# Rotary turn of retention heads: a permutation product on TensorE or two half-partition instructions on VectorE

## What is computed

```
half = t.shape[-1] // 2
ang = positions.astype(jnp.float32)[..., None] * freq
...
t1 = t[..., :half].astype(jnp.float32)
t2 = t[..., half:].astype(jnp.float32)
return jnp.concatenate([t1 * cos - t2 * sin, t1 * sin + t2 * cos], axis=-1).astype(t.dtype)
...
q = _rotary(q, positions)
k = _rotary(k, positions) * (dh ** -0.5)
...
s = jnp.einsum('bhid,bhjd->bhij', qc, kc) * decay_intra
```

## Time and profile before

| | us |
|---|---|
| median of 3 runs | 3482.7 |
| lowest and highest | 3477.58, 3488.25 |
| the profiled execution: its time | 3476.79 |
| the profiled execution: its span | 3474.8 |
| TensorE busy | 3343.4 |
| VectorE busy | 1779.1 |
| ScalarE busy | 1196.5 |
| GpSimd busy | 411.3 |

### The profile page before, as it was taken

How to read it: one execution, slowest core, us unless ns; L and a number is a source line. 1 busy time by engine, 2 the same in 40 slices (tenths; PEclk the granted TensorE clock), 3 DMA queues, 4 the chain that set the end, 5 groups by cost and what they waited for, 6 DMA issues and landing times.

```text
span 3474.8 us, 44141 instructions
## 1 busy us (share of the span) xinstructions
PE 3343.4 (96%) x18394; PEld 2598.4 (75%) x18394; DVE 1779.1 (51%) x2532; ACT 1196.5 (34%) x1884; POOL 411.3 (12%) x318
## 2 busy tenths in 40 slices
PE   5999999899999899999999999999999999999999
PEld 4776778576677788887777777888777887678887
DVE  6854454744436744336767554333554334563333
ACT  3344432433443422224333342222343223442221
POOL 0000011000000311002322111100101011011110
PEclk8999999999999999999999999999999999999999
DMA  5631122222122333324200013332322323023232
GB/s 208 214 110 61 49 97 91 72 80 61 55 76 71 103 103 91 97 86 124 69 18 3 26 47 118 94 95 85 100 79 91 96 90 94 13 61 97 91 97 85
DMA packets 83909, 295.44 MB, mean 85 GB/s; under 512 B 9472, under 2 KB 12800, under 8 KB 81664
## 3 DMA queue, kind: packets, MB, share of 16 engines
q1 hardware_dynamic: 78384, 270.61, 24.9%
q10 hardware_dynamic: 5328, 22.02, 1.8%
HBM read 283.94 MB, written 8.65 MB: 84 GB/s over the span
## 4 chain that ended last, share of the span: by engine, by line
PE 85%; DVE 9%; ACT 2%; issue 2%; POOL 1%; DMA 0%; ACTq 0%; DVEq 0%; POOLq 0%
PE acc L475 68%; DVE w_lo L386 1%; PE acc L1464 1%; PE acc L3219 1%; PE acc L2445 1%; ACT w_hi L379 1%; DVE square_sums L2904 1%; PE aux L1745 1%; PE aux L3183 1%; PE acc L1778 1%; DVE ssd_ex L1366 1%; PE acc L2449 1%; PE acc L2435 1%; PE aux L1765 1%; PE aux L2402 1%
## 5 line engine op out<-in xcount | busy, mean ns | idle before, releaser
L475 PE MATMUL acc<-op_hi,w_hi 128*128 128x512 f32 x2624 | 1099.2, 419 | 37.9 <-DVE w_lo L386 16.8
L475 PE MATMUL acc<-op_lo,w_hi 128*128 128x512 f32 x2624 | 1040.4, 396 | 0.0
L475 PE MATMUL acc<-op_hi,w_lo 128*128 128x512 f32 x2624 | 1040.0, 396 | 0.0
L379 ACT ACTIVATE w_hi<-raw 128x1024 fp32r<-128x1024 f32 (+2 forms) x476 | 494.8, 1039 | 1582.4 <-PE acc L475 1554.6
L386 DVE TENSOR_TENSOR w_lo<-raw,w_hi 128x1024 fp32r<-128x1024 f32 (+2 forms) x476 | 576.8, 1212 | 289.9 <-ACT w_hi L379 289.5
L475 PEld LDWEIGHTS acc<-op_hi,w_hi 128*128 128x128 f32 x2624 | 495.2, 189 | 219.3 <-issue 82.7
L475 PEld LDWEIGHTS acc<-op_hi,w_lo 128*128 128x128 f32 x2624 | 495.2, 189 | 119.5
L475 PEld LDWEIGHTS acc<-op_lo,w_hi 128*128 128x128 f32 x2624 | 496.3, 189 | 115.0 <-issue 11.5
L475 PE MATMUL acc<-ffn_hi,w_hi 128*128 128x512 f32 x800 | 316.7, 396 | 0.0
L475 PE MATMUL acc<-ffn_lo,w_hi 128*128 128x512 f32 x800 | 316.3, 395 | 0.0
L475 PE MATMUL acc<-ffn_hi,w_lo 128*128 128x512 f32 x800 | 316.3, 395 | 0.0
(11 more groups left out here) (580 smaller groups left out, 3915.6 us busy)
## 6 DMA issues: line engine op xcount, KB each, us to landing
raw<-in_w SPq DMA_DIRECT2D x436, 512.0 KB, 3.5
late_ada<-in_ada ACTq DMA_DIRECT2D x32, 512.0 KB, 3.8
raw<-in_w SPq DMA_DIRECT2D x32, 384.0 KB, 3.1
ada<-in_ada ACTq DMA_DIRECT2D x4, 1024.0 KB, 14.9
ada<-in_ada SPq DMA_DIRECT2D x4, 1024.0 KB, 21.8
x_mid<-x SPq DMA_DIRECT2D x16, 256.0 KB, 3.4
x<-x_mid SPq DMA_DIRECT2D x2, 2048.0 KB, 7.8
skew<-rel_rows SPq DMA_DIRECT2D x12, 192.0 KB, 2.8
```

The lines of the kernel that those rows point to most:

```text
L379: act.activation(self.w_hi[g % 2][:, 0:k, :], self.raw[s][:, 0:k, :], ACT.Copy).then_inc(self.split_hi.handle, 1)
L475: mm = pe.matmul(self.bank(s, g), w[:, k, :], a[:, k, 0:s.n], start=(k == 0 and q == 0), stop=(k == k_tiles - 1 and q == 2))
```

## The change

The product with `rot` goes, and with it the signal `swapped` and the use of the banks `aux[0]` and `aux[1]` by the rotation. VectorE instead reads `qk` itself, in two instructions of 64 partitions each: one reads the second half of the head and the second half of `sin` and writes minus their product to the first 64 partitions of `part2`, and one reads the first halves and writes their product to partitions 64 to 127. The first of them waits for what the product with `rot` waited for (queries and keys there, attention done). The addition and POOL's product stay. VectorE's model times lie 2.3 apart now instead of 1.6, and begin at 0.4. POOL's stay 1.6 apart. The score's stays at `start + 20`.

```diff
@@ class Ret, pe
-        def rotations():
-            for j in range(2 * RET_HEADS):
-                yield self.start + 1.6 * j
-                if j == 0:
-                    pe.wait_ge(*self.qk_ready)
-                    pe.wait_ge(*self.fox.done())
-                if j >= 2:
-                    pe.wait_ge(*self.sined.ge(j - 1))
-                pe.matmul(core.aux[j % 2][:, :], core.c("rot"), qk[:, j, :], start=True,
-                          stop=True).then_inc(*self.swapped.inc())
...
@@ class Ret, dve
         def rotations():
             for j in range(2 * RET_HEADS):
-                yield self.start + 1.6 * j + 1.4
-                dve.wait_ge(*self.swapped.ge(j + 1))
+                yield self.start + 2.3 * j + 0.4
+                if j == 0:
+                    dve.wait_ge(*self.qk_ready)
+                    dve.wait_ge(*self.fox.done())
                 if j >= 2:
                     dve.wait_ge(*self.turned.ge(j - 1))
-                dve.tensor_tensor(self.part2[:, j % 2, :], core.aux[j % 2][:, :], core.sin[:, :],
+                upper, lower = slice(HD, P), slice(0, HD)
+                dve.scalar_tensor_tensor(out=self.part2[lower, j % 2, :], in0=qk[upper, j, :], scalar=-1.0,
+                                         in1=core.sin[upper, :], op0=ALU.mult, op1=ALU.mult)
+                dve.tensor_tensor(self.part2[upper, j % 2, :], qk[lower, j, :], core.sin[lower, :],
                                   ALU.mult).then_inc(*self.sined.inc())
                 dve.wait_ge(*self.sined.ge(j + 1))
                 dve.wait_ge(*self.cosed.ge(j + 1))
```

More of the change, by code:

```diff
@@ L1872, in __init__ @@
         self.loaded = core.share("ret_decay", 16)
-        self.swapped, self.cosed, self.sined, self.turned = (core.share("rot_" + s, n) for s in (
-            "swapped", "cos", "sin", "done"))
+        self.cosed, self.sined, self.turned = (core.share("rot_" + s, n) for s in ("cos", "sin", "done"))
         self.units = [(h, jt) for h in range(RET_HEADS) for jt in range(NT)]
@@ L1972, in spreads @@
                 mm.then_inc(*self.spread.inc())
-        return rotations(), scores(), values(), means(), spreads()
+        return scores(), values(), means(), spreads()
     def norm_time(self, h):
```

## The result

| | before | after |
|---|---|---|
| median of 16 runs each, us | 3482.57 (3477.29 to 3500.5) | 3500.03 (3490.27 to 3508.95) |
| ratio | | 1.0049, interval 1.0038 to 1.0059 |
| span of the profiled execution, us | 3474.8 | 3499.4 |
| mean granted clock of TensorE | 0.983 | 0.977 |
| L379 to L379 around the rotations, layer 1 and layer 2, us | 31.06, 31.04 | 37.90, 37.91 |

What follows compares the result with a forecast made beforehand. It took TensorE as the bound before, and VectorE's eight rotations after: 17.04 us of rotations, 4.12 POOL, 2.40 copies and 2.52 tile work put the score 6.5 us later; +13.2 us for two layers gave 3496, range 3486 to 3504.

Steps and rivals of the forecast that it cites:

- VectorE becomes the bound: In each layer's rotations, the score waits for VectorE's eighth rotation, 26.08 us after VectorE is free at 492.95.
- A rotation at 2.13 us: On VectorE, two half instructions at 0.68 us and an addition at 0.69, without overlapping starts: 2.13 us, before 1.33.
- POOL's turns at 4.12 us: Per layer, VectorE's two-input instructions take turns with POOL's cosine product and lose 4.12 us in all.
- rival of POOL and the half instructions passing each other: Half instructions run beside POOL undelayed: 3.0 us a layer, 3489, or 3485.5 with overlapping starts; chance 0.18.
- TensorE idle in a new place: Before the score, TensorE waits nearly 12 us at the third unit of transposes for the first copy, L1883.
- Nothing for the clock at the score: TensorE at half clock after its wait reaches the score half a microsecond late; nothing was taken for this.
- The rival with more lost: Low clock past the score (3502.5) or POOL costing its whole 1.12 us in all six cases (3501); chance 0.14.
- +6.5 at the score, +6.6 at the first product with the values: In each layer the score moves from 512.66 to 519.2, the first product with the values from 515.56 to 522.2.
- the same distance from the score to the layer's end: Behind the score TensorE has the same work as before, so the distance to the layer's end stays unchanged.
- The relief counts for nothing: TensorE's saved 8 us a layer gain nothing, since the score waits for VectorE; the opposing rival, 3467, had chance 0.02.
- The sum carried over to the median: Two layers' +13.2 us, added to the median of 3482.7, give 3495.9; the difference carries over unchanged.
- VectorE is 2.7 us behind TensorE: In the kernel before, VectorE's eighth rotation ends at 509.93, 2.7 us before the score that waits for it.

Runs made afterwards that it cites:

- pool_no_read: The changed kernel with POOL's cosine product replaced by a memset of the same tile: ratio to before 1.0020, layers 2.80 and 2.83 us longer than before.
- same_half: The changed kernel with both half instructions reading and writing partitions 0 to 63, the turn left out: each layer 5.58 us longer than before; no ratio.
- one_full: The changed kernel with one 128-partition instruction in place of the two half ones, the swap left out: ratio to before 1.0013, layers +1.40 and +1.64 us.
- old_pace: The changed kernel with VectorE's model times as before the change (1.6 apart, from 1.4): ratio to before 1.0059, layers +8.22 and +9.40 us.
- by_head2: The changed kernel, all work kept, rotations ordered by head and spread out, copies given room: ratio to before 0.9967, layers -7.35 and -7.33 us.
- before_idle: The kernel before with two unused reciprocals on VectorE ahead of its fifth rotation, nothing taken off TensorE: ratio to before 1.0044, layers +7.96 and +8.45 us.

## Why the prediction came out as it did

Point by point, by the prediction's steps:

- **VectorE becomes the bound.** Right. It predicted 26.08 us from VectorE's being free to the end of the eighth rotation; in after it is 494.90 (the end of L386) to 520.99, 26.09. That it fits to 0.01 us is luck: POOL's turns were 0.1 us less than summed, and the rest 0.1 us more (22.06 in pool_no_read for 21.96).
- **A rotation at 2.13 us.** Right. From 494.93 to 497.07 it is 2.14. The half instruction has 0.69 us for the 0.68 assumed, and same_half shows that the missing overlap is due to the change of partitions.
- **POOL's turns at 4.12 us.** Right within 0.1 us: 4.03 by after against pool_no_read (26.09 - 22.06). By the rows, L2014 lost 0.99 us (0.98 predicted) in rotation 2, POOL took 1.79 (1.7 to 1.8), and L2012 of rotation 7 lost 1.28 - 0.69 = 0.59 (0.63). One reading was ill chosen: L2021 at 501.86 was not beside POOL, which had ended at 501.39. The L2021 at 504.32, inside POOL's 503.34 to 505.52, shows that it never waited, with 0.68 us. The rival of POOL and the half instructions passing each other falls.
- **TensorE idle in a new place.** Right: nearly 12 us predicted, 11.81 measured, and for the copy that was named.
- **Nothing for the clock at the score.** Right, but by a narrow margin. The prediction's own arithmetic had TensorE half a microsecond too late and let that pass, and TensorE came 0.3 us early for two reasons that it didn't have: the slow matmuls lasted 5.6 us for the 6.65 of the earlier trace rows, and the two units of transposes were 0.43 us each for 0.60. one_full and old_pace show what happens without the margin: the score comes 1.3 and 2.1 us behind VectorE (in old_pace 0.3 of them would be there at full clock too, 515.04 + 5.8 against 520.5).
- **The rival with more lost.** The measured 3500 lies close to its 3501 and 3502.5, but neither of its mechanisms came about. The clock was back at full before the score, and POOL cost 4.0 us and not 6 x 1.12.
- **+6.5 at the score, +6.6 at the first product with the values.** The score stands at 521.05 - 1.95 = 519.10 (519.2 predicted), the product with the values at 524.26 - 1.95 = 522.31 (522.2), 6.75 us later than before; the layer ends 6.85 later. So the sign "the same distance from the score to the layer's end" didn't hold to the tenth: 8.17 us for 7.77, 0.3 of them up to the product with the values. The 0.25 us that are missing a layer make 13.7 instead of 13.2.
- **The relief counts for nothing.** Right in this order of work: one_full has it alone and is not faster. by_head2 shows that this holds for the order and not for the chip. There the relief is worth 7.3 us a layer.
- **The sum carried over to the median.** This term was mis-sized. The prediction took the rest of the program to be as long in both, so 13.2 us in all, and the medians lie 17 apart. 13.7 are shown, and the interval begins just below them. The other 3.4 are within the spread, or are the clock in stretches that the change doesn't touch, for which the sum had no term.

One sentence of the prediction was too simple: that VectorE is 2.7 us behind TensorE. before_idle shows that this was so at the score only. At the products with `rot` there was no slack, and 6.4 of the 6.5 us of delay on VectorE reached TensorE. The sum was not hurt, since it followed VectorE to the end and didn't use the slack as a cover. Two side figures of the rivals are slightly off and enter nothing: with overlapping starts 3.0 - 1.8 us a layer give 3485, not 3485.5, and 504.8 - 492.95 less 4.9 leaves 0.87 us a rotation, not 0.8.

## What to carry to other kernels

Work taken off the engine that bounds the kernel is worth nothing if it goes to one that runs without a gap in the same stretch; count that engine's instructions from the moment it is free to the one that is waited for, with the turns it has to take with a neighbour. An instruction on half the partitions cost as much here as one on all (0.69 us both), so two for one is double. If the moved work is in the way, look first which results are needed when: here the same instructions, in the order of their use and with gaps for the copies that TensorE waits for, turned a loss of 6.85 us a layer into a gain of 7.3.

## What the runs showed of the hardware

- VectorE with two SBUF inputs on 64 partitions and POOL take turns just as on 128: L2014 lasted 1.65 to 1.68 us for 0.69, POOL's product 1.76 to 1.79 for 1.28. This agrees with the Trainium skill, SBUF — State Buffer, section Who interferes with whom. A memset on POOL in the same place took 0.524 us and delayed nothing (pool_no_read).
- Turning to the other half of the partitions costs 0.10 to 0.11 us an instruction (0.60 to 0.70, 0.61 to 0.72).
- After 11.8 us of waiting TensorE worked at 1.2 GHz for 5.6 us; after 7.2 us of waiting for 4.7 us (before_idle, 510.16 to 514.89). From 491 to 500, ahead of the first wait, its clock was 1.00.
- I hadn't expected that a stretch with the same 499 matmuls takes 89.7 to 99.0 us from one execution to another (thirteen traces of nine kernels that are the same there), in step with a granted clock of 0.90 to 0.79. The same kernel, traced three times, varied by up to 2.8 us there. A change of a few microseconds is read from the distance between two marks around it, which repeated here within 0.03 us.
